# Two transposed probability tiles ahead of the next unit's scores, in the attention of the last two query groups

## The chip, the cores and the metric

The kernel runs on one core of a Trainium2 chip. The metric is the device time of one execution in microseconds (us). All tensors are float32. TensorE (PE) multiplies, VectorE (DVE) and ScalarE (ACT) do the element work, GpSimd (POOL) helps a little, SyncE (SP) issues the loads.

## The reference

Two blocks follow each other on 2048 tokens of width 1024. The change touches only the attention of the second block, which is, cut to what matters:

```python
# q_lat: (tokens, 8 heads, 128), c: latent keys (tokens, 128), w_uv: (8, 128, 64)
s_idx = ...                                  # index scores of a query against all keys
_, sel = lax.top_k(where(causal, s_idx, -inf), 256)
lg_s = q_lat @ c[sel].T * scale + rel_bias   # 8 heads
lg_m = q_lat @ c_meta.T * scale + rel_bias   # 16 meta tokens
p = softmax(concatenate([lg_m, lg_s]))
out = (p_meta @ c_meta + p_sel @ c[sel]) @ w_uv
```

The kernel doesn't gather the 256 keys: it computes the scores against all keys up to the query's block and adds a mask (`sel`, 0 or -1e30) that leaves out the keys that are not chosen.

## The kernel before, in words

The program is written out by hand, engine by engine, and the engines meet by semaphores alone. The 2048 tokens go in four groups of 512 queries (`g` = 0 to 3), each of four blocks of 128 queries (block `i` = 4g to 4g+3). For every group the second block's projections and scans run first (`second_steps`), then the attention, then the output projection.

The attention of a group is a loop over 32 **units**: a unit is one block `i` and one of 8 heads `h`. Block `i` has 128(i+1) keys, so a unit of block 8 is 1152 keys wide and one of block 15 is 2048 wide. A unit passes these stations:

1. PE: the scores S. `far` tiles of up to 512 keys (L1920) and a `near` tile of the last 256 keys (L1924). Each goes to one PSUM bank. The first head of a block is preceded by eight small products for the meta tokens (`score_m`, L1914).
2. DVE: it adds mask or bias while it copies a tile to `probs` and takes the maximum (L1530, L1537), then reduces the maxima and writes their negative to `stat` (L1544, L1545). After that it does one part of the key selection of the next block (`beside`).
3. ACT: one exp over the whole row, in place in `probs`, with the row's sum (L1058 and the read of the accumulator behind it). The semaphore `probs2_made` is raised by the last of them.
4. PE: transposes of the probabilities, 128 keys at a time, up to four to a PSUM tile (`p2_t`, L1944). A unit has `prob_tiles(i)` such tiles: 3 for blocks 8 to 11 and 4 for blocks 12 to 15. They are called T0, T1, T2, T3 here.
5. ACT: it copies each transposed tile to `prob_t` (L1052).
6. PE: the value products (L1952), called V0 to V3 here. Vc needs the copy of Tc.

The units are pipelined by one. In iteration `u` PE first computes the scores of unit `u`, then does stations 4 and 6 for unit `u-1` in the order T0, T1, V0, T2, V1, (T3, V2,) and the last V. ACT goes through the copies of unit `u-1` and then the exp of unit `u`; it takes its instructions in the order written. At two places in a block's turn there is more in an iteration: the transpose and product for the meta tokens (`pm_t`, L1930 and L1932) when a block ended two units earlier, and the transposes of the finished output (`o2_t`, four at L1966) when it ended three units earlier.

PSUM has six banks for tiles (`RING = 6`), given out in one fixed order over the whole program (`schedule`, here `dsa_tiles`). `claim` makes PE wait until the tile six places before was drained. `prob_t` has three slots (`PT_SLOTS = 3`).

Of the kernel before, what the change touches and what calls it, by code (L numbers as in the profile page):

```python
# [220 lines left out]
def keys_of(i):  # L221
    return (i + 1) * P
# [25 lines left out]

def prob_tiles_before(i, h):
    return H2 * sum(prob_tiles(b) for b in range(i)) + h * prob_tiles(i)  # L250
# [25 lines left out]
def dsa_tiles(g):  # L276
    units = dsa_units(g)
    for u in range(len(units) + 4):
        if u < len(units):
            i, h = units[u]  # L280
            if h == 0:
                yield ("score_m", i)
            yield from [("far", i, h, c) for c in range(len(far_chunks(i)))]
            yield ("near", i, h)
        if ended(units, u, 2) is not None:
            yield ("pm_t", ended(units, u, 2))
        if 1 <= u <= len(units):
            i, h = units[u - 1]
            yield from [("p2_t", i, h, c) for c in range(prob_tiles(i))]
# [70 lines left out]
def program(nc, A, out_t):  # L360
# [9 lines left out]
    with ctx:  # L370
# [410 lines left out]
        def _(act):  # L781
# [145 lines left out]

            def act_level(g, pair, lev):
# [6 lines left out]
            for g in range(G):  # L935
# [103 lines left out]
                for u in range(len(units) + 4):  # L1039
                    if ended(units, u, 2) is not None:  # L1040
# [3 lines left out]
                    if 1 <= u <= len(units):  # L1044
                        i, h = units[u - 1]
                        for c in range(prob_tiles(i)):
                            m = prob_tiles_before(i, h) + c
                            wide_ = min(TB, keys_of(i) - c * TB)
                            wait_tile(act, "p2_t", i, h, c)
                            if m >= PT_SLOTS:  # L1050
                                act.wait_ge(pv2_done, m - PT_SLOTS + 1)
                            drains(A_(prob_t[:, m % PT_SLOTS, 0:wide_], bank("p2_t", i, h, c)[:, 0:wide_], ACT.Copy), "p2_t", i, h, c)  # L1052
# [522 lines left out]
        def _(pe):  # L1575
# [221 lines left out]
            for g in range(G):  # L1797
# [107 lines left out]
                units = dsa_units(g)  # L1905
                for u in range(len(units) + 4):
                    if u < len(units):
# [25 lines left out]
                    if 1 <= u <= len(units):  # L1933
                        i, h = units[u - 1]
                        n = H2 * BG * g + u - 1
                        pe.wait_ge(probs2_made, n + 1)
                        if h == 0 and i >= 2:
                            pe.wait_ge(o2_scaled, i - 1)
                        count = prob_tiles(i)

                        def transposes2(c):
                            claim("p2_t", i, h, c)
                            for k in range(c * BG, min(c * BG + BG, i + 1)):
                                ins = nc.tensor.transpose(bank("p2_t", i, h, c)[:, (k % BG) * P:(k % BG + 1) * P],  # L1944
                                                          probs[:, (n % 2) * S + k * P:(n % 2) * S + (k + 1) * P], ident[:])
                            ins.then_inc(tile_ready, 1)

                        def values2(c):
                            wait_drained(pe, "p2_t", i, h, c)
                            m = prob_tiles_before(i, h) + c  # L1950
                            for k in range(c * BG, min(c * BG + BG, i + 1)):
                                ins = M(o_acc[i % 2][:, h * DH2:(h + 1) * DH2], prob_t[:, m % PT_SLOTS, (k % BG) * P:(k % BG + 1) * P],  # L1952
                                        v2[:, k, h * DH2:(h + 1) * DH2], start=(h == 0 and k == 0), stop=False, skip_group_check=True)
                            ins.then_inc(pv2_done, 1)

                        transposes2(0)
                        for c in range(1, count):
                            transposes2(c)
                            values2(c - 1)
                        values2(count - 1)  # L1960
# [117 lines left out]
```

## Time and profile before

| | |
|---|---|
| median of three runs | 4444.76 us (4441.53 to 4445.15) |
| the profiled execution | 4463.69 us, of which the span from first to last instruction is 4461.9 us |
| PE busy | 3973.0 us, 89% of the span |
| PE's weight loads (PEld) | 2294.7 us, 51% |
| DVE busy | 1802.1 us, 40% |
| ACT busy | 1477.2 us, 33% |
| mean granted TensorE clock | 0.932 |
| attention of group 2 (32 units) | from about 3345 to 3562 us of the span |
| attention of group 3 (32 units) | from about 4073 to 4353 us of the span |

A row of the timeline gives the start in us from the span's start, the time taken, the engine, the line, the operation, what it writes and reads, how many instructions are merged in the row, and in brackets how long the engine had been idle and who released it. A float32 matrix product stands as two instructions, so "x8" at L1952 is four value products and "x8" at L1944 is the eight transposes of T0 and T1. PE overlaps instructions, and the ends are modelled; so the text reads starts against starts.

### The profile page before, as it was taken

Reading aid. Unit: us, or ns where it says so; the run is one execution under the profiler, and the core shown is the slowest. Engines: PE = TensorE matmul, PEld = TensorE weight load, DVE = VectorE, ACT = ScalarE, POOL = GpSimd, SP = SyncE. Lnnn points to the kernel's source line nnn. Section 1 sums busy time; section 2 is a strip of 40 time slices with the busy share of each in tenths; the row PEclk is TensorE's granted clock in tenths of the full one; section 3 lists DMA queues with packets and bytes.
Section 4 is the critical chain, followed back from the end, with each engine's and each line's share of the span. In section 5 each row is a group of like instructions: output and inputs, shape, how many; then the busy total and the mean of one; then the engine's idle time right before and its main releaser. Section 6 shows DMA issues by size and latency. Waiting matters only on the chain.

```text
span 4461.9 us, 41285 instructions
## 1 busy us (share of the span) xinstructions
PE 3973.0 (89%) x15538; PEld 2294.7 (51%) x15538; DVE 1802.1 (40%) x4182; ACT 1477.2 (33%) x2457; POOL 268.7 (6%) x328
## 2 busy tenths in 40 slices
PE   7899999999999999799789787897889997687996
PEld 3346645644664464354554445644447743345773
DVE  3313222322322221227422576425776414777631
ACT  1213222312331231212312454314664413675441
POOL 0010001000000100011101011001011001011000
PEclk8999999999999999799699898998889998898998
DMA  4120022013002200411022010111100111010001
GB/s 145 57 94 6 15 78 73 1 48 106 13 10 66 71 1 19 139 50 52 1 86 75 26 48 1 62 57 50 47 19 1 58 57 52 22 48 1 1 24 53
DMA packets 70920, 204.16 MB, mean 46 GB/s; under 512 B 6297, under 2 KB 7873, under 8 KB 70465
## 3 DMA queue, kind: packets, MB, share of 16 engines
q1 hardware_dynamic: 61344, 183.67, 12.3%
q10 hardware_dynamic: 9376, 17.84, 1.1%
q8 instruction: 125, 2.05, 0.2%
q14 instruction: 75, 0.61, 0.0%
HBM read 184.69 MB, written 16.79 MB: 45 GB/s over the span
## 4 chain that ended last, share of the span: by engine, by line
PE 75%; ACT 11%; DVE 9%; issue 3%; DMA 1%; SPq 0%; POOL 0%; ACTq 0%; DVEq 0%; POOLq 0%
PE bank L1593 32%; PE o_acc L1952 6%; PE o_acc L1720 5%; PE bank L1688 5%; ACT ql L925 4%; PE bank L1920 4%; PE bank L1692 3%; PE bank L1815 3%; PE bank L1713 2%; PE bank L1944 2%; PE bank L1601 2%; PE bank L1850 2%; ACT prob_t L1052 2%; PE bank L1640 1%; PE bank L1924 1%
## 5 line engine op out<-in xcount | busy, mean ns | idle before, releaser
L1593 PE MATMUL bank<-group_even,weights 128*128 128x512 f32 x1376 | 610.3, 602 | 20.3 <-DMA weights<-in_w_in_kv 12.3
L1593 PE MATMUL bank<-group_odd,weights 128*128 128x512 f32 x1376 | 612.3, 603 | 9.4 <-ACT tmp L912 5.9
L1593 PE MATMUL bank<-y_all,weights 128*128 128x512 f32 x1024 | 452.2, 604 | 14.6 <-DMA weights<-in_w_out 8.2
L1593 PEld LDWEIGHTS bank<-group_even,weights 128*128 128x128 f32 x1376 | 264.3, 194 | 345.6 <-issue 341.3
L1593 PEld LDWEIGHTS bank<-group_odd,weights 128*128 128x128 f32 x1376 | 265.3, 195 | 337.4 <-issue 333.1
L1593 PEld LDWEIGHTS bank<-y_all,weights 128*128 128x128 f32 x1024 | 197.8, 194 | 264.3 <-issue 264.3
L1952 PE MATMUL o_acc<-v,prob_t 128*128 128x64 f32 x2176 | 293.2, 283 | 45.4 <-ACT prob_t L1052 45.4
L1178 DVE CUSTOM_DVE_ANT_0 probs<-bank,mask 128x512 f32<-128x512 f32 x256 | 161.6, 687 | 417.8 <-PE bank L1692 417.8
L1952 PEld LDWEIGHTS o_acc<-v,prob_t 128*128 128x128 f32 x2176 | 271.9, 198 | 79.9 <-ACT prob_t L1052 79.9
L1052 ACT ACTIVATE prob_t<-bank 128x512 f32<-128x512 f32 (+3 forms) x320 | 160.2, 532 | 398.9 <-PE bank L1944 398.9
L867 ACT ACTIVATE prob_t<-bank 128x512 f32<-128x512 f32 x256 | 145.9, 596 | 430.3 <-PE bank L1713 430.3
L1720 PE MATMUL o_acc<-val,prob_t 128*128 128x128 f32 x2048 | 270.3, 280 | 16.0 <-ACT prob_t L867 16.0
L1720 PEld LDWEIGHTS o_acc<-val,prob_t 128*128 128x128 f32 x2048 | 247.3, 191 | 31.2 <-ACT prob_t L867 31.2
L1530 DVE CUSTOM_DVE_ANT_0 probs<-bank,sel 128x512 f32<-128x512 f32 (+3 forms) x256 | 147.6, 595 | 227.3 <-PE bank L1920 223.9
L1688 PE MATMUL bank<-k_nope,q_nope 128*128 128x512 f32 x512 | 230.7, 593 | 0.0
L1920 PE MATMUL bank<-c_t,ql 128*128 128x512 f32 (+3 forms) x512 | 215.4, 549 | 10.3 <-DVE s_meta L1520 7.0
L1944 PE MATMUL bank<-ident,probs 128*128 128x128 f32 x1088 | 164.2, 282 | 27.7 <-ACT probs L1058 27.7
L925 ACT ACTIVATE ql<-index,mids 128x384 bf16<-128x384 f32 (+2 forms) x144 | 133.3, 927 | 124.2 <-DVE mids L1359 113.2
L1850 PE MATMUL bank<-probs 128*128 128x128 f32 x640 | 102.0, 326 | 77.8 <-DVE probs L1419 75.3
L1944 PEld LDWEIGHTS bank<-ident,probs 128*128 128x128 f32 x1088 | 136.9, 151 | 50.6 <-ACT probs L1058 30.0
L1058 ACT ACTIVATE probs<-probs,stat 128x128 f32<-128x128 f32 (+15 forms) x128 | 153.2, 1197 | 24.6 <-DVE stat L1545 23.9
L1850 PEld LDWEIGHTS bank<-probs 128*128 128x128 f32 x640 | 96.4, 236 | 104.4 <-DVE probs L1419 92.9
(340 smaller groups left out, 5002.5 us busy)
## 6 DMA issues: line engine op xcount, KB each, us to landing
weights<-in_w_in SPq DMA_DIRECT2D x101, 512.0 KB, 3.5
weights<-in_w_in_q SPq DMA_DIRECT2D x64, 512.0 KB, 3.5
weights<-in_w_out SPq DMA_DIRECT2D x64, 512.0 KB, 3.5
weights<-in_w_i SPq DMA_DIRECT2D x20, 512.0 KB, 3.5
group_even<-in_x_t SPq DMA_DIRECT2D x8, 1024.0 KB, 7.9
group_odd<-in_x_t SPq DMA_DIRECT2D x8, 1024.0 KB, 9.0
group_even<-x_t SPq DMA_DIRECT2D x8, 1024.0 KB, 8.0
group_odd<-x_t SPq DMA_DIRECT2D x8, 1024.0 KB, 7.3
```

Source lines behind the costliest of these rows:

```text
L925: A_(tested_act[:, m % 2, 0:share], index_of(BG * g + b)[:, n - share:n], ACT.Sign, scale=-1.0, bias=mids[:, b, r:r + 1], accum_out=signs[ ...
L1052: drains(A_(prob_t[:, m % PT_SLOTS, 0:wide_], bank("p2_t", i, h, c)[:, 0:wide_], ACT.Copy), "p2_t", i, h, c)
L1058: A_(p, p, ACT.Exp, bias=stat[:, 8 + n % 2:9 + n % 2], accum_out=sums2[:, i % 2, h:h + 1]).then_inc(probs2_made, 1)
L1178: drains(V.tensor_tensor_reduce(out=probs[:, (n % 2) * S + c * TB:(n % 2) * S + (c + 1) * TB], in0=bank("score", i, h, c)[:], in1=mask[:, ...
L1530: drains(V.tensor_tensor_reduce(out=probs[:, base + at:base + at + wide_], in0=bank("far", i, h, c)[:, 0:wide_], in1=sel[:, i % 2, at:at + ...
L1593: ins = M(bank(*name)[:], ring[n % SLOTS][:, k * P:(k + 1) * P], rhs[:, k, :], start=(k == 0), stop=(k == chunks - 1))
L1688: M(bank("score", i, h, c)[:], q_nope[:, h, b * P:(b + 1) * P], k_nope[:, h, c * TB:(c + 1) * TB], start=True, stop=False)
L1720: ins = M(o_acc[i % 2][:, h * P:(h + 1) * P], prob_t[:, m % PT_SLOTS, k * P:(k + 1) * P], val[:, c * BG + k, h * P:(h + 1) * P], start=(c ...
L1850: ins = M(bank(*st, e)[:, cols], keys[:, e, cols], queries[:, e, cols], start=True, stop=True)
L1920: M(bank("far", i, h, c)[:, 0:wide_], query, c_t[:, at:at + wide_], start=True, stop=True).then_inc(tile_ready, 1)
L1944: ins = nc.tensor.transpose(bank("p2_t", i, h, c)[:, (k % BG) * P:(k % BG + 1) * P], probs[:, (n % 2) * S + k * P:(n % 2) * S + (k + 1) * ...
L1952: ins = M(o_acc[i % 2][:, h * DH2:(h + 1) * DH2], prob_t[:, m % PT_SLOTS, (k % BG) * P:(k % BG + 1) * P], v2[:, k, h * DH2:(h + 1) * DH2], ...
```

## The change

For blocks 8 to 15, which are the attention of groups 2 and 3, a number `lead_of(i)` of 2 is introduced (0 for the earlier blocks, which stay as they were). In iteration `u`, PE now waits for the probabilities of unit `u-1` first and makes T0 and T1; then come the scores of unit `u`; then V0, T2, V1, V2 (three tiles) or V0, T2, V1, T3, V2, V3 (four). No instruction is added or dropped. The order in which PSUM banks are given out, and the place of the `pm_t` copy among ACT's copies, follow.

```diff
+def lead_of(i):
+
+    return 2 if i >= 2 * BG else 0
...
 def dsa_tiles(g):
     units = dsa_units(g)
     for u in range(len(units) + 4):
+        if 1 <= u <= len(units):
+            i, h = units[u - 1]
+            yield from [("p2_t", i, h, c) for c in range(prob_tiles(i))][:lead_of(i)]
         if u < len(units):
...
         if 1 <= u <= len(units):
             i, h = units[u - 1]
-            yield from [("p2_t", i, h, c) for c in range(prob_tiles(i))]
+            yield from [("p2_t", i, h, c) for c in range(prob_tiles(i))][lead_of(i):]
...
@@ ACT
                 for u in range(len(units) + 4):
+                    if 1 <= u <= len(units):
+                        for c in range(lead_of(units[u - 1][0])):
+                            transposed(*units[u - 1], c)
                     if ended(units, u, 2) is not None:
...
                     if 1 <= u <= len(units):
-                        i, h = units[u - 1]
-                        for c in range(prob_tiles(i)):
...
+                        for c in range(lead_of(units[u - 1][0]), prob_tiles(units[u - 1][0])):
+                            transposed(*units[u - 1], c)
@@ PE
                 for u in range(len(units) + 4):
+                    if 1 <= u <= len(units):
+                        i, h = units[u - 1]
+                        pe.wait_ge(probs2_made, H2 * BG * g + u)
+                        for c in range(lead_of(i)):
+                            transposes2(u - 1, c)
                     if u < len(units):
...
                     if 1 <= u <= len(units):
                         i, h = units[u - 1]
-                        n = H2 * BG * g + u - 1
-                        pe.wait_ge(probs2_made, n + 1)
                         if h == 0 and i >= 2:
                             pe.wait_ge(o2_scaled, i - 1)
...
+                        count, lead = prob_tiles(i), lead_of(i)
+                        if lead == 0:
...
+                        else:
+                            for c in range(lead, count):
+                                values2(u - 1, c - lead)
+                                transposes2(u - 1, c)
+                            for c in range(count - lead, count):
+                                values2(u - 1, c)
```

In groups 0 and 1, where `lead_of` is 0, the instructions keep their order, but the wait for `probs2_made` of unit `u-1` now stands ahead of the scores of unit `u` there too. Before, it stood behind them. On PE at a unit of block 0 the program before has, with the semaphores that an instruction waits for:

```order
L1924 MATMUL bank<-c_t,ql 128x128 [waits drained5]
L1944 MATMUL bank<-ident,probs 128x128 [waits drained0,probs2_made]
L1952 MATMUL o_acc<-v,prob_t 128x64 [waits drained0]
L1924 MATMUL bank<-c_t,ql 128x128 [waits drained1]
L1944 MATMUL bank<-ident,probs 128x128 [waits drained2,probs2_made]
L1952 MATMUL o_acc<-v,prob_t 128x64 [waits drained2]
```

and the changed one:

```order
L1962 MATMUL bank<-c_t,ql 128x128 [waits drained5,probs2_made]
L1926 MATMUL bank<-ident,probs 128x128 [waits drained0]
L1935 MATMUL o_acc<-v,prob_t 128x64 [waits drained0]
L1962 MATMUL bank<-c_t,ql 128x128 [waits drained1,probs2_made]
L1926 MATMUL bank<-ident,probs 128x128 [waits drained2]
L1935 MATMUL o_acc<-v,prob_t 128x64 [waits drained2]
```

The wait for `probs2_made` went from the transpose (L1944) up to the scores (L1962 in the new file); nothing else moved there.

On PE, in the middle of block 14 of group 3, the order before is this. L1920 and L1924 are the scores, L1944 the transposes (x8 is T0 and T1), L1952 the value products.

```order
L1920 MATMUL bank<-c_t,ql 128x512 x3
L1920 MATMUL bank<-c_t,ql 128x128
L1924 MATMUL bank<-c_t,ql 128x256
L1944 MATMUL bank<-ident,probs 128x128 x8
L1952 MATMUL o_acc<-v,prob_t 128x64 x4
L1944 MATMUL bank<-ident,probs 128x128 x4
L1952 MATMUL o_acc<-v,prob_t 128x64 x4
L1944 MATMUL bank<-ident,probs 128x128 x3
L1952 MATMUL o_acc<-v,prob_t 128x64 x7
```

At the same place the changed program has this. Its L1926 is the transposes, L1935 the value products, L1958 and L1962 the scores.

```order
L1926 MATMUL bank<-ident,probs 128x128 x8
L1958 MATMUL bank<-c_t,ql 128x512 x3
L1958 MATMUL bank<-c_t,ql 128x128
L1962 MATMUL bank<-c_t,ql 128x256
L1935 MATMUL o_acc<-v,prob_t 128x64 x4
L1926 MATMUL bank<-ident,probs 128x128 x4
L1935 MATMUL o_acc<-v,prob_t 128x64 x4
L1926 MATMUL bank<-ident,probs 128x128 x3
L1935 MATMUL o_acc<-v,prob_t 128x64 x7
```

The scores moved from ahead of T0 to between T1 and V0. So what lies between the scores of a unit and its own T0 is now one row of values less the scores of another unit, and what lies between T0 and V0 is more by those scores.

At the start of group 3's attention PE has this before (L1914 is the meta tokens' scores of block 12).

```order
L1914 MATMUL bank<-c_meta,ql 128x16 x8
L1920 MATMUL bank<-c_t,ql 128x512 x2
L1920 MATMUL bank<-c_t,ql 128x384
L1924 MATMUL bank<-c_t,ql 128x256
L1920 MATMUL bank<-c_t,ql 128x512 x2
L1920 MATMUL bank<-c_t,ql 128x384
L1924 MATMUL bank<-c_t,ql 128x256
L1944 MATMUL bank<-ident,probs 128x128 x8
L1952 MATMUL o_acc<-v,prob_t 128x64 x4
```

And in the changed program, where L1952 is the meta tokens' scores:

```order
L1952 MATMUL bank<-c_meta,ql 128x16 x8
L1958 MATMUL bank<-c_t,ql 128x512 x2
L1958 MATMUL bank<-c_t,ql 128x384
L1962 MATMUL bank<-c_t,ql 128x256
L1926 MATMUL bank<-ident,probs 128x128 x8
L1958 MATMUL bank<-c_t,ql 128x512 x2
L1958 MATMUL bank<-c_t,ql 128x384
L1962 MATMUL bank<-c_t,ql 128x256
L1935 MATMUL o_acc<-v,prob_t 128x64 x4
```

The scores of the group's second unit stood ahead of the first transposes; now they stand behind them. Group 2 starts in the same way.

## Rows read from the trace of the kernel before

**Rows 1.** Timeline of one unit of block 15 in group 3.

```profile
4318.48 3.23 PE L1920 MATMUL bank<-c_t,ql 128*128 128x512 f32 x8
...
4321.97 1.04 PE L1944 MATMUL bank<-ident,probs 128*128 128x128 f32 x8
...
4323.02 0.15 DVE L1545 TENSOR_SCALAR stat<-m 128x1 f32<-128x1 f32 x1
4323.26 1.10 PE L1952 MATMUL o_acc<-v,prob_t 128*128 128x64 f32 x8 [0.25 <-ACT prob_t L1052]
...
4324.20 0.60 PE L1944 MATMUL bank<-ident,probs 128*128 128x128 f32 x4
4324.64 1.00 PE L1952 MATMUL o_acc<-v,prob_t 128*128 128x64 f32 x8
...
4325.48 0.61 PE L1944 MATMUL bank<-ident,probs 128*128 128x128 f32 x4
...
4326.62 1.99 ACT L1058 ACTIVATE probs<-probs,stat 128x2048 f32<-128x2048 f32 x1
4327.72 1.51 PE L1920 MATMUL bank<-c_t,ql 128*128 128x512 f32 x3
```

**Rows 2.** Timeline of one unit of block 8 in group 2.

```profile
3378.57 1.10 PE L1952 MATMUL o_acc<-v,prob_t 128*128 128x64 f32 x8 [0.25 <-ACT prob_t L1052]
...
3380.69 1.72 PE L1920 MATMUL bank<-c_t,ql 128*128 128x512 f32 x4
3381.14 0.19 ACT L1058 ACTIVATION_READ_ACCUMULATOR probs<-probs,stat 128x1 f32 x1
```

**Rows 3.** Timeline of one unit of block 12 in group 3.

```profile
4117.24 1.10 PE L1952 MATMUL o_acc<-v,prob_t 128*128 128x64 f32 x8 [0.25 <-ACT prob_t L1052]
...
4120.64 1.94 PE L1920 MATMUL bank<-c_t,ql 128*128 128x512 f32 x4
4121.52 0.19 ACT L1058 ACTIVATION_READ_ACCUMULATOR probs<-probs,stat 128x1 f32 x1
```

**Rows 4.** Timeline of group 3's last unit, which no further scores precede.

```profile
4341.74 1.10 PE L1952 MATMUL o_acc<-v,prob_t 128*128 128x64 f32 x8 [0.25 <-ACT prob_t L1052]
...
4346.99 0.19 ACT L1058 ACTIVATION_READ_ACCUMULATOR probs<-probs,stat 128x1 f32 x1
...
4347.23 1.09 PE L1944 MATMUL bank<-ident,probs 128*128 128x128 f32 x8 [0.88 <-ACT probs L1058]
...
4348.57 0.66 PE L1952 MATMUL o_acc<-v,prob_t 128*128 128x64 f32 x4 [0.25 <-ACT prob_t L1052]
```

**Rows 5.** Timeline of PE in the first two units of group 2.

```profile
3351.51 1.97 PE L1944 MATMUL bank<-ident,probs 128*128 128x128 f32 x8 [2.52 <-ACT probs L1058]
...
3353.31 1.97 PE L1952 MATMUL o_acc<-v,prob_t 128*128 128x64 f32 x8
...
3357.31 3.30 PE L1920 MATMUL bank<-c_t,ql 128*128 128x512 f32 x4
...
3361.09 1.04 PE L1944 MATMUL bank<-ident,probs 128*128 128x128 f32 x8
```

**Rows 6.** Timeline of PE in the first unit of group 3.

```profile
4078.19 1.10 PE L1944 MATMUL bank<-ident,probs 128*128 128x128 f32 x8 [0.57 <-ACT probs L1058]
```

**Rows 7.** Timeline between two units of block 0 in group 0.

```profile
2182.36 0.74 PE L1924 MATMUL bank<-c_t,ql 128*128 128x128 f32 x2
2182.45 0.19 ACT L1058 ACTIVATION_READ_ACCUMULATOR probs<-probs,stat 128x1 f32 x1
```

**Rows 8.** Timeline between two units of block 4 in group 1.

```profile
2748.21 0.20 ACT L1058 ACTIVATION_READ_ACCUMULATOR probs<-probs,stat 128x1 f32 x1
2748.66 0.86 PE L1920 MATMUL bank<-c_t,ql 128*128 128x384 f32 x2
```

**Rows 9.** Two stretches: PE, PEld, DVE, ACT, POOL busy (x), clock, DMA share, GB/s.

```profile
4080.00:4352.00 272.00, 262.30 (x1715) 207.21 (x1714) 139.30 (x408) 124.91 (x195) 15.43 (x24) 1.00 0.04 13
2732.00:2897.00 165.00, 146.72 (x847) 111.19 (x846) 76.06 (x278) 60.20 (x130) 15.32 (x24) 0.93 0.11 39
```

More of the change, by code:

```diff
@@ L926, in signs_of, with transposed @@
                        accum_out=signs[:, b, r:r + 1]).then_inc(signs_summed, 1)
+            def transposed(i, h, c):
+                m = prob_tiles_before(i, h) + c
+                wide_ = min(TB, keys_of(i) - c * TB)
+                wait_tile(act, "p2_t", i, h, c)
+                if m >= PT_SLOTS:
+                    act.wait_ge(pv2_done, m - PT_SLOTS + 1)
+                drains(A_(prob_t[:, m % PT_SLOTS, 0:wide_], bank("p2_t", i, h, c)[:, 0:wide_], ACT.Copy), "p2_t", i, h, c)
             def act_level(g, pair, lev):
@@ L1905, in _, with transposes2, values2 @@
                 units = dsa_units(g)
-                for u in range(len(units) + 4):
+                def transposes2(u, c):
+                    i, h = units[u]
+                    n = H2 * BG * g + u
+                    claim("p2_t", i, h, c)
+                    for k in range(c * BG, min(c * BG + BG, i + 1)):
+                        ins = nc.tensor.transpose(bank("p2_t", i, h, c)[:, (k % BG) * P:(k % BG + 1) * P],
+                                                  probs[:, (n % 2) * S + k * P:(n % 2) * S + (k + 1) * P], ident[:])
+                    ins.then_inc(tile_ready, 1)
+                def values2(u, c):
+                    i, h = units[u]
+                    wait_drained(pe, "p2_t", i, h, c)
+                    m = prob_tiles_before(i, h) + c
+                    for k in range(c * BG, min(c * BG + BG, i + 1)):
+                        ins = M(o_acc[i % 2][:, h * DH2:(h + 1) * DH2], prob_t[:, m % PT_SLOTS, (k % BG) * P:(k % BG + 1) * P],
+                                v2[:, k, h * DH2:(h + 1) * DH2], start=(h == 0 and k == 0), stop=False, skip_group_check=True)
+                    ins.then_inc(pv2_done, 1)
+                for u in range(len(units) + 4):
+                    if 1 <= u <= len(units):
[3 more added lines that the diff above has]
+                            transposes2(u - 1, c)
                     if u < len(units):
@@ L1934, in _ @@
                         i, h = units[u - 1]
-                        n = H2 * BG * g + u - 1
-                        pe.wait_ge(probs2_made, n + 1)
                         if h == 0 and i >= 2:
                             pe.wait_ge(o2_scaled, i - 1)
[L1939 to L1960, printed above, removed]
+                        count, lead = prob_tiles(i), lead_of(i)
+                        if lead == 0:
+                            transposes2(u - 1, 0)
+                            for c in range(1, count):
+                                transposes2(u - 1, c)
+                                values2(u - 1, c - 1)
+                            values2(u - 1, count - 1)
+                        else:
+                            for c in range(lead, count):
+                                values2(u - 1, c - lead)
+                                transposes2(u - 1, c)
+                            for c in range(count - lead, count):
+                                values2(u - 1, c)
                     over = ended(units, u, 3)
```

6 lines of the change are left out of this document (removed).

## The prediction

> **What bounds the kernel now.** I read the table of busy times first, then the timeline of single units in each group's attention, then the busy table of whole stretches. PE is the engine to watch: it is busy 89% of the span, and in group 3's attention (the stretch from 4080) 262.3 of 272 us, with the clock at 1.00 [rows 9]. A unit of block 15 shows the whole turn, read start to start [rows 1]: scores 4318.48 to 4321.97 (3.49 us), T0 and T1 up to V0 at 4323.26 (1.29), then V0, T2, V1, T3, V2, V3 up to the next scores at 4327.72 (4.46), 9.24 us in all. PE's one wait in it is at V0, for ACT's copy of T0: 0.25 us idle, in blocks 8 and 12 as well [rows 1 to 3]. The exp of the scores just made starts at 4326.62, behind the copy of T3, and runs on into PE's next scores; nobody waits for it. So two latencies stand in a unit: the copy of T0, which PE sees, and the exp, which the next scores cover.
>
> **The change part by part.** In groups 2 and 3 it exchanges the two: the scores cover the copy, and the value products alone must cover the exp. In groups 0 and 1 it only moves the wait for the exp ahead of the scores.
>
> *What is won in a unit of groups 2 and 3.* T2's four transposes give the bare pace, 4324.20 to 4324.64 = 0.44 us, so T0 and T1 take 0.88 where 1.29 pass now: 0.41 won. V0, begun after a stall, takes 0.94 up to T2, while V1 takes 0.84, 4324.64 to 4325.48 [rows 1]: 0.10 more won, as V0 will follow the scores without a pause. Together 0.51.
>
> *What is lost there.* T0 of the next unit comes straight after the last V. It needs the exp, and the exp comes behind the copy of the last T, since ACT takes its work in order; that copy hangs on V0's start in the same iteration, so I measure from there. The trace already has this order once in each group: behind the last unit's T and V there are no further scores. In block 15, V0 starts at 4341.74, the exp is done at 4346.99 + 0.19 = 4347.18, and T0 starts at 4347.23, 0.05 later and 5.49 after V0 [rows 4]. The T and V work ends 4.46 after V0 [rows 1]: the wait is 1.03. In block 12 the exp is done 4.47 after V0 (4121.71), the work at 3.40 [rows 3]; with the 0.05 the wait is 1.12. In block 8 it is 2.76 (3381.33) + 0.05 against 2.12 [rows 2]: 0.69. T0 after a wait has its first weights to load: 1.34 to V0, against 1.29 [rows 4, 1], so 0.05 more. I take the mean of the ends for group 3, 1.08, and for group 2, with the same fall of 0.09 over its blocks, 0.65.
>
> *Counts.* A group has 32 units. The last gap before T0 waits already, and the first unit is costed below; this leaves 30 waits in group 3. In group 2 the half clock at the start, where V and T take 4.00 us [rows 5], covers the exp once more, which leaves 29. Waits: 30 x 1.08 + 29 x 0.65 = 51.3. At six places the four transposes of `o2_t` (0.44, by T2's pace) lie in the gap: -2.6. At six block changes the exp is 128 keys wider, 1.99 x 128 / 2048 = 0.12 [rows 1]: +0.7. That makes +49.4. Won: 59 x (0.51 - 0.05) = -27.1. Together +22.3.
>
> *The starts of groups 2 and 3.* The scores of unit 1 were made while PE waited for the first exp; now they follow it. In group 2 the clock is at half after the pause: T0 and T1 take 1.80, and block 8's scores 3.78, 3357.31 to 3361.09 [rows 5], where full clock would give 3.49 x 1152/2048 = 1.96. In the new order: T0 at 3351.51, scores from 3353.3, V0 at 3357.1, T0 of unit 1 at 3361.1, then at full clock 0.93 and 1.96, V0 at 3364.0. Now that V0 comes 1.29 after 3361.09: +1.6. In group 3 PE was busy with unit 1's scores ahead of T0 at 4078.19 [rows 6], so V0 came after a normal 1.3. Now PE idles until T0, so T0, T1 and block 12's scores follow a pause as in group 2: at full clock 0.93 + 2.84, at half 1.80 + 5.5, that is +2.4 or +5.9. Group 2's rows, whose scores six us behind the pause still took twice their time, are the nearer: +5.0.
>
> *Groups 0 and 1.* In block 0 the exp is done at 2182.45 + 0.19 = 2182.64, while the scores behind it start at 2182.36 [rows 7]. With 0.05 they will start 0.33 later, and DVE and ACT, which set this turn, don't catch up: 7 x 0.33 = 2.3. In block 4 the exp is done at 2748.41 and the scores start at 2748.66 [rows 8]: 0.20 to spare, no cost. At both groups' starts unit 1's scores are uncovered as above; by width at half clock that is about 0.6 in group 0 and 2.1 in group 1. With 0.2 for other places of group 0, +5.2. If the 0.20 of group 1 were gone and 0.1 missing, 31 units would cost 3.1 more.
>
> *Costed at nothing.* PSUM banks: with 6, 8 or 9 tiles to a unit, the tile six places before is always one that DVE or ACT took before the exp in question or during the scores. DVE in groups 2 and 3: `stat` is ready 1.20 us after the scores' end, which is T0's start now (4323.17 against 4321.97) and V0's in the new order; the exp starts 3.36 after V0 in block 15 [rows 1]. In block 8 it starts 1.4 after V0 (its end, 2.76, less 1.3), so the cover is 0.1 to 0.2; each 0.1 that is missing costs up to 6 us over 60 units. DVE's selection part behind `stat` has the exp, T0, T1 and the first scores to hide in, over 3 us even in block 8. `pm_t` and its wait stand ahead of V0 as before.
>
> *Sum.* 22.3 + 1.6 + 5.0 + 5.2 = +34.1 us. On the profiled execution this is 4463.7 + 34.1 = 4497.8; the runs' median is 18.9 lower, so 4444.8 + 34.1 = **4478.9 us**, 0.77% slower.
>
> **A rule against the change.** In group 3's attention the clock is at 1.00 with PE busy 96%; in group 1's (from 2732), where PE is busy 146.7 of 165 us, 89%, it is 0.93 [rows 9]. The new waits bring groups 2 and 3 to about 88%. With two levels, a mean of 0.93 is half clock for 14% of the time. The Trainium skill, TensorE: Matmul & The Clock Gate, section on the second HAM failure mode, says that PE idling briefly but often between groups of products makes the clock swing between its levels. By that rule the loss would be larger than my sum; group 1's row agrees with it, group 3's doesn't contradict it. What it would do here is the second rival.
>
> **The rivals.**
> 1. *As summed*: 4478.9, between 4468 and 4490 from the start in group 3 and the small terms. Chance 0.67.
> 2. *The clock falls too.* With group 1's 0.93, 14% of 470 us, 66 us, pass at half, which costs about half of it, +33: 4512; if the clock falls only at the block changes, +5 to +20. I put it at 4500. For it: the busy share. Against it: the scores here are wider than group 1's. Chance 0.15.
> 3. *DVE or ACT is late as well*, by 0.2 to 0.3 us a unit in the narrow blocks, where the spare is 0.1 to 0.2: +10 to +18, about 4493. Chance 0.05.
> 4. *The waits are smaller than I read them*, half of 1.08 and 0.65 or so, if the turn settles at another phase: 25 us less, 4454. Against it: the trace has the new order at 4347.23, with just the wait computed [rows 4]. Chance 0.08.
> 5. *The other side: the copy's wait goes and nothing takes its place.* The exp would have to be done within the V and T work, so to start at least 1.03 us sooner in block 15, ahead of T3's copy. Then 59 x 0.51 = 30.1 are won and 11.8 lost at the starts and in group 0: 4426. It is a gain from a mean wait below 0.26 (59 x 0.26 = 27.1 - 11.8). Against it is ACT's order, which has the exp last. Chance 0.05.
>
> **How the numbers follow.** The predicted time is the first case's. The range 4465 to 4502 takes in its own range, most of the third and half of the second; the fourth, the fifth and the worst of the clock stay outside, about 0.2. A measurement of this kernel can tell 0.2%, 9 us, from no change. Faster is the fifth case, 0.05; same is part of the fourth, 0.04; slower is the rest, 0.91.
>
> **What the profile after would show.** At the transposes' line the exp (ACT `probs`) should stand as PE's releaser about 60 times, with 0.9 us idle in group 3 and about 0.5 in group 2 (idle by the page, 0.88 at 4347.23 for 1.03 start to start [rows 4]). The wait for `prob_t` at V0 should be left in groups 0 and 1 and at the last units. A unit of block 15 should last 9.24 + 1.03 + 0.05 - 0.51 = 9.81 us, of block 12 0.66 more than now, of block 8 0.23 more. In block 0 the scores should wait for the exp, in block 4 not. The clock should be 1.00 in groups 2 and 3 apart from their starts. Another releaser, or a clock that falls inside a group, would make the prediction wrong.

## The result and the profile after

The changed kernel took 4496.95 us in the median of four executions (4482.10 to 4499.11), against 4444.95 us for the kernel before beside it: ratio 1.0111, 95% interval 1.0089 to 1.0134. It is slower, by 52 us where 34 were forecast. A second comparison, told below, gave 1.0072 (1.0050 to 1.0095), 32 us; of its ten executions of the change one took 13905.6 us, at a mean granted clock of 0.394, and is left out. The profiled execution took 4482.10 us, span 4480.3.

The page after, PE's busy row and clock row first, then two groups (busy, mean ns | idle before, and its releaser):

```profile
PE 3957.1 (88%) x15538; PEld 2292.7 (51%) x15538; DVE 1802.3 (40%) x4182; ACT 1478.3 (33%) x2457; POOL 268.7 (6%) x328
...
PEclk9999999999999999789699899998889998888998
...
L1935 PE MATMUL o_acc<-v,prob_t 128*128 128x64 f32 x2176 | 281.3, 277 | 30.4 <-ACT prob_t L943 30.4
...
L1926 PE MATMUL bank<-ident,probs 128*128 128x128 f32 x1088 | 167.8, 286 | 71.2 <-ACT probs L1072 71.0
```

PE's waits from 3330 to 4400, the attention of groups 2 and 3 and what lies between (us in total, times, longest):

```profile
PE bank L1926 <- ACT probs L1072: 71.0, 61, 14.6
...
PE o_acc L1935 <- ACT prob_t L943: 0.5, 2, 0.3
```

The exchange is in these two rows. The wait for the copy at the value products (L1935) is gone but for two, 0.5 us in all; in its place stand 61 waits for the exp at the transposes (L1926). The longest of them, 14.6 and 13.7, are the two group starts, where PE waited before as well, though partly with scores in between.

Timeline of a unit of block 15, which answers to [rows 1]:

```profile
4333.04 1.00 PE L1935 MATMUL o_acc<-v,prob_t 128*128 128x64 f32 x8
4333.88 0.61 PE L1926 MATMUL bank<-ident,probs 128*128 128x128 f32 x4
...
4335.81 0.60 ACT L943 ACTIVATE prob_t<-bank 128x512 f32<-128x512 f32 x1 [0.69 <-PE bank L1926]
4336.30 1.99 ACT L1072 ACTIVATE probs<-probs,stat 128x2048 f32<-128x2048 f32 x1
4338.19 0.19 ACT L1072 ACTIVATION_READ_ACCUMULATOR probs<-probs,stat 128x1 f32 x1
4338.44 1.09 PE L1926 MATMUL bank<-ident,probs 128*128 128x128 f32 x8 [0.88 <-ACT probs L1072]
...
4339.37 3.17 PE L1958 MATMUL bank<-c_t,ql 128*128 128x512 f32 x8
...
4342.81 1.00 PE L1935 MATMUL o_acc<-v,prob_t 128*128 128x64 f32 x8
```

Read start to start: V0 to the next T0 takes 5.40 us. V0 now takes 0.84 like V1, so the T and V work is 4.36, and PE waits 1.04. T0 starts 0.06 after the exp's read of the accumulator ends (4338.38). T0 and T1 take 0.93, the scores 3.44, and V0 follows at 4342.81 with no wait: the copies of T0 and T1, 1.08 us from 4339.13, are done while the scores run. The turn is 9.77 us, where [rows 1] gave 9.24.

The same in block 12 (V0, then T0 behind its wait):

```profile
4112.57 1.00 PE L1935 MATMUL o_acc<-v,prob_t 128*128 128x64 f32 x8
...
4117.00 1.09 PE L1926 MATMUL bank<-ident,probs 128*128 128x128 f32 x8 [0.97 <-ACT probs L1072]
```

And in block 8:

```profile
3370.30 1.00 PE L1935 MATMUL o_acc<-v,prob_t 128*128 128x64 f32 x8
...
3373.02 1.09 PE L1926 MATMUL bank<-ident,probs 128*128 128x128 f32 x8 [0.54 <-ACT probs L1072]
```

The start of group 3's attention, which answers to [rows 6]:

```profile
4073.98 1.97 PE L1926 MATMUL bank<-ident,probs 128*128 128x128 f32 x8 [14.55 <-ACT probs L1072]
...
4075.74 3.95 PE L1958 MATMUL bank<-c_t,ql 128*128 128x512 f32 x6
...
4079.96 1.00 PE L1935 MATMUL o_acc<-v,prob_t 128*128 128x64 f32 x8
```

PE stood still for 14.55 us, T0 and T1 then took 1.76, twice the pace of 0.88, and the scores 4.22, between the 2.84 of full and the 5.5 of half clock: the clock came back while they ran. V0 is 5.98 us behind T0, where it was 1.3 behind. So the start costs 4.7.

The start of group 2's attention, which answers to [rows 5]:

```profile
3342.18 1.97 PE L1926 MATMUL bank<-ident,probs 128*128 128x128 f32 x8 [13.71 <-ACT probs L1072]
3343.94 3.19 PE L1958 MATMUL bank<-c_t,ql 128*128 128x512 f32 x4
...
3347.78 1.18 PE L1935 MATMUL o_acc<-v,prob_t 128*128 128x64 f32 x8
...
3350.68 1.09 PE L1926 MATMUL bank<-ident,probs 128*128 128x128 f32 x8 [0.54 <-ACT probs L1072]
```

V0 comes 5.60 us behind T0, all of it at half clock (0.50 from 3342 to 3348). From 3348 to 3349 the granted clock is 0.93, so the V and T work behind it runs at full clock, and T0 of the next unit follows 2.90 after V0, behind a wait.

Between two units of block 0, which answers to [rows 7]:

```profile
2180.95 0.19 ACT L1072 ACTIVATION_READ_ACCUMULATOR probs<-probs,stat 128x1 f32 x1
2181.19 0.79 PE L1962 MATMUL bank<-c_t,ql 128*128 128x128 f32 x2
```

The exp ends at 2181.14 and the scores start 0.05 later. The turn is 2.19 us (these scores start at 2181.19, the next at 2183.38), against 1.80 before. In block 4 it is 3.58 as before.

Two stretches after, of groups 3 and 2 (columns as in [rows 9]):

```profile
4100.00:4360.00 260.00, 233.91 (x1505) 185.98 (x1506) 121.95 (x360) 110.31 (x172) 15.43 (x24) 0.99 0.00 1
3365.00:3550.00 185.00, 171.12 (x1118) 137.76 (x1118) 94.29 (x308) 80.82 (x141) 15.40 (x24) 1.00 0.04 12
```

From its first exp to its last, group 2 lasts 211.1 us (206.9 before) and group 3 293.4 (268.7 before). Together that is 28.9 us more.

### The profile page after: what moved, and what is told of

Read it like the earlier page. It is cut to its first block, busy times and chain, and to the rows that moved or that the text cites. A ratio compares the mean times of both kernels' runs of the same rounds, so it can differ in the third digit from the quotient of the medians.

```text
span 4480.3 us, 41299 instructions
## 1 busy us (share of the span) xinstructions
PE 3957.1 (88%) x15538; PEld 2292.7 (51%) x15538; DVE 1802.3 (40%) x4182; ACT 1478.3 (33%) x2457; POOL 268.7 (6%) x328
## 4 chain that ended last, share of the span: by engine, by line
PE 73%; ACT 12%; DVE 10%; issue 3%; DMA 1%; SPq 0%; POOL 0%; DVEq 0%; ACTq 0%; POOLq 0%
PE bank L1607 31%; PE o_acc L1734 5%; PE bank L1702 5%; ACT ql L933 5%; PE bank L1958 4%; PE o_acc L1935 3%; PE bank L1926 3%; PE bank L1706 3%; PE bank L1829 3%; ACT probs L1072 2%; PE bank L1727 2%; PE bank L1615 2%; PE bank L1864 2%; PE bank L1654 1%; PE bank L1962 1%
## 5 line engine op out<-in xcount | busy, mean ns | idle before, releaser
L1935 PE MATMUL o_acc<-v,prob_t 128*128 128x64 f32 x2176 | 281.3, 277 | 30.4 <-ACT prob_t L943 30.4
L1935 PEld LDWEIGHTS o_acc<-v,prob_t 128*128 128x128 f32 x2176 | 272.1, 195 | 55.3 <-ACT prob_t L943 49.4
L1926 PE MATMUL bank<-ident,probs 128*128 128x128 f32 x1088 | 167.8, 286 | 71.2 <-ACT probs L1072 71.0
L1958 PE MATMUL bank<-c_t,ql 128*128 128x512 f32 (+3 forms) x512 | 210.9, 541 | 13.2 <-ACT probs L1072 13.2
L1926 PEld LDWEIGHTS bank<-ident,probs 128*128 128x128 f32 x1088 | 132.6, 151 | 92.6 <-ACT probs L1072 81.0
L1727 PE MATMUL bank<-ident,probs 128*128 128x128 f32 x1024 | 146.1, 275 | 3.3 <-ACT probs L880 3.3
```

The lines of the kernel that those rows point to most:

```text
L1727: ins = nc.tensor.transpose(bank(*name)[:, k * P:(k + 1) * P], probs[:, col:col + P], ident[:])
L1958: M(bank("far", i, h, c)[:, 0:wide_], query, c_t[:, at:at + wide_], start=True, stop=True).then_inc(tile_ready, 1)
```

## The experiments

Two theories stood against each other. **The chain**: V0, the T's that follow it, the copy of the last of them, then the exp, then the next T0, and PE waits for what its own work doesn't cover. **The clock**: the new waits, in groups 0 and 1 above all, bring the granted clock down, which would explain the surplus of the first comparison over the sum. A turn below is the time from the start of one exp to the start of the next; a steady turn is one away from a group's start and from the changes of block.

**The wait moved, without the lead.** In every group the wait for the exp stands ahead of the scores, and the tiles stay where they were.

```diff
-    return 2 if i >= 2 * BG else 0
+    return 0
```

> The change without its main part: no tile goes ahead in any group, but the wait for the exp stands ahead of the next unit's scores in all four groups. If unhidden exps are what costs (theory A), groups 2 and 3 pay the same here as in the change, without what V0 wins: per unit S, T, V and then a wait. From V0 the exp is done as before (5.49 us in block 15, 4.52 in block 12, 2.81 in block 8 against 4.46, 3.40, 2.12), so about +1.0, +1.1 and +0.7 a unit, +50 us in groups 2 and 3, +5 in groups 0 and 1 and +10 at the starts: +60 us, 1.35%. If it was the exchange with the copy's wait that mattered (theory B: the order of T and S as such costs), this kernel should be near the one before, +5 to +10.

Measured: 4528.4 us (4 executions), ratio 1.0177 (1.0153 to 1.0202), the kernel before on this chip at 4450.8. PE in block 15 of that kernel, two waits in one turn:

```profile
4345.14 1.10 PE L1935 MATMUL o_acc<-v,prob_t 128*128 128x64 f32 x8 [0.25 <-ACT prob_t L943]
...
4350.64 2.84 PE L1958 MATMUL bank<-c_t,ql 128*128 128x512 f32 x6 [0.88 <-ACT probs L1072]
```

Both latencies stand open here: 5.50 from V0 to the scores, and the copy's 0.25 besides. The steady turns are 6.15 us in block 8 and 10.33 in block 15, against 5.59 and 9.77 in the changed kernel. So the lead of two tiles wins 0.56 us a unit (0.51 forecast), and the exp's wait costs 0.75 to 1.17 with what hangs on it (block 8 and 12). The change as a whole is the lead's gain less a larger loss.

The time is more than was expected: 1.35% lies below the interval. Groups 2 and 3 last 234.9 and 317.6 us from first exp to last, 76.9 more than in the kernel before. Of these, 16.8 stand in eight turns that are 1.7 or 3.4 us longer than at full clock; behind the starts the two groups have 34 us at half clock. Two stretches behind the starts (columns as in [rows 9], granted clock 0.96):

```profile
4125.00:4385.00 260.00, 230.17 (x1385) 173.64 (x1384) 115.81 (x340) 99.90 (x156) 15.42 (x24) 0.96 0.00 1
3365.00:3550.00 185.00, 166.54 (x998) 126.78 (x998) 85.98 (x276) 71.94 (x127) 15.44 (x24) 0.96 0.04 12
```

So with both waits open the clock did fall inside the groups. The profile is one, but all four executions lie above 4526 us. What is left, 60 us, is what was expected of the groups and their starts (50 and 10).

**The lead, without the moved wait in groups 0 and 1.**

```diff
-                        pe.wait_ge(probs2_made, H2 * BG * g + u)
+                        if lead_of(i) > 0:
+                            pe.wait_ge(probs2_made, H2 * BG * g + u)
...
+                        if lead_of(i) == 0:
+                            pe.wait_ge(probs2_made, H2 * BG * g + u)
```

> The change without its side effect: T0 and T1 go ahead in groups 2 and 3, and in groups 0 and 1 the wait for the exp is where it was. Theory A by the prediction's terms: groups 2 and 3 cost 22.3 + 6.6 = +29 us, and in groups 0 and 1 nothing, so 5 us less than the change. Theory C says that what the change's median has over the sum (52 against 34 us) is the clock in groups 0 and 1, pushed to its lower level by the moved wait in block 0: then this kernel is about 20 us faster than the change, near +29 with a group 0 like the one before. If the excess comes from groups 2 and 3, it stays near +47.

Measured: 4478.4 us (6 executions), ratio 1.0063 (1.0039 to 1.0088). Groups 2 and 3 have the turns of the changed kernel to 0.01 us, block 0 has its 1.80 again. The ratio's 28 us are near the 29 that the chain gave. By itself this spoke for the clock theory too, since it lies 18.6 us below the first median of the change. The next two runs speak otherwise.

**The changed kernel again, in more executions.**

> The changed kernel itself, with more runs, beside the moved wait alone and on the chip of the other experiments. If what exceeded the sum (52 us measured against 34 forecast) was chance in the clock of single runs, the median comes near 4451 + 34 = 4485 us (ratio 1.0077). If the moved wait in groups 0 and 1 costs through the clock, it stays near 4497 us (ratio 1.011), that is 18 us above the kernel that has the same order in groups 2 and 3 but the old wait in groups 0 and 1 (4478.4).

Measured: 4482.8 us, ratio 1.0072 (1.0050 to 1.0095), from nine executions of 4472.6 to 4498.8. That is near the expected 1.0077, and 0.0009 above the lead alone. The first comparison's four executions of the change, and its four of the kernel before, lie within the range of the single executions here, the highest 0.3 us above it, so its surplus can be chance; a difference between the chips that the two ran on isn't excluded.

**The moved wait in groups 0 and 1 alone**, the rest as before.

```diff
-    return 2 if i >= 2 * BG else 0
+    return 0
...
-                        pe.wait_ge(probs2_made, H2 * BG * g + u)
+                        if i < 2 * BG:
+                            pe.wait_ge(probs2_made, H2 * BG * g + u)
...
+                        if i >= 2 * BG:
+                            pe.wait_ge(probs2_made, H2 * BG * g + u)
```

> The kernel before, with the wait for the probabilities moved ahead of the scores in groups 0 and 1 alone; groups 2 and 3 stay as they were. By the prediction's sum: +5.2 us, ratio 1.0012 (block 0's unit 2.19 instead of 1.80, the first scores of the two groups uncovered). If this wait pulls the clock down as well: +15 to +20 us, ratio 1.0035 to 1.0045, with more of group 0 and 1 at half clock in the profile.

Measured: 4457.5 us (12 executions) against 4452.4, ratio 1.0007 (0.9989 to 1.0026). In block 0 the first turn rose from 1.23 to 2.09, the five steady ones from 1.80 to 2.19 and the one into block 1 from 5.88 to 6.27, 3.15 us over the block. The clock theory's 1.0035 to 1.0045 is outside the interval: as an explanation of the surplus it falls. The forecast 5.2 us are inside, and so is no cost at all.

The moved wait does change where the clock is low, though. In the five profiles that have it (this one, the one without the lead, two of the changed kernel and, below, one with half of the exp) group 0 lasts 103.5 to 106.1 us from first exp to last and group 1 145.5 to 152.0. In the eight with the old wait group 0 lasts 91.2 to 115.1, and group 1 152.2 in seven and 147.3 in one. The two groups together take 249.0 to 258.0 us (252.9 in the mean) against 243.5 to 266.0 (252.2).

**Second profiles of both kernels.**

> A second profile of the changed kernel. Its steady units should be the same within 0.01 us (5.59, 8.15, 9.77), as they belong to the order; what differs from the first profile (span 4480.3) should stand in the stretches at half clock alone: near the beginning of each group's attention, at block changes and in blocks 1 and 2.

> A second profile of the kernel before. Its steady units should be the same within 0.01 us (5.40, 7.54, 9.24); its span may differ from 4461.9 by 10 to 25 us, all of it at half clock in groups 0 and 1 and at block changes, if the spread from run to run is the clock's.

Measured: the change 4486.5 us (span 4484.6), the kernel before 4447.3 (span 4445.5, 16.4 less than in its first profile). The steady turns of both agree with their first profiles within 0.01 us. In the kernel before, group 0's attention in the first profile:

```profile
2174.00:2265.00 91.00, 77.19 (x315) 58.95 (x316) 39.79 (x181) 27.18 (x84) 16.55 (x27) 0.61 0.07 24
```

The same stretch in the second profile:

```profile
2174.00:2265.00 91.00, 74.09 (x391) 56.73 (x390) 46.04 (x212) 33.91 (x97) 15.41 (x24) 0.81 0.08 25
```

One program, one stretch of 91 us, and once 315 and once 391 matmul instructions done, at a clock of 0.61 and 0.81. From first to last exp group 0 lasts 105.3 and 91.3 us, which is 14.0 of the 16.4 us between the spans. In group 3 of the changed kernel two stretches at half clock, at 4208 and 4218, make the turns at two block changes 12.38 and 12.51 us long; the second profile has 10.70 and 10.84 there, and 1.68 more in two other turns. The kernel before has such turns as well (10.19 for 8.49 and 11.24 for 9.54 in its second profile). They aren't the change's alone, but it may bring more of them. In groups 2 and 3, behind the half clock of the starts, four profiles with the old order have none, two, none and one (the kernel before twice, the moved wait in groups 0 and 1 alone, and the kernel before with half of the exp, below). Both profiles of the changed kernel and that of the lead alone have two, and the kernel with the first units in the old order, also below, has three, one of them 10.2 us long. So few profiles don't settle it, and at 1.7 us for 3.4 at half clock it is little.

**Half of the exp, in the changed kernel and in the kernel before.** Both leave out half of the exponentials.

```diff
-                        p = probs[:, (n % 2) * S:(n % 2) * S + keys_of(i)]
+                        p = probs[:, (n % 2) * S:(n % 2) * S + (keys_of(i) if i < 2 * BG else (i + 2) // 2 * P)]
...
+                    return k if i < 2 * BG else k // 2
```

> The changed kernel with the exp over about half of the row in groups 2 and 3 (blocks 8 to 15; the transposes read that half twice), so it leaves out half of the exponentials. The exp is shorter by 0.82 ns a key: 0.42 us in block 8, 0.63 in block 12, 0.84 in block 15. If PE's wait is for the end of the exp, the units shrink by just that, to 5.17, 7.52 and 8.93 us, and the waits for the exp to 0.27, 0.49 and 0.19; some 37 us in all. If the wait came from the copies or from DVE, the units would stay at 5.59, 8.15 and 9.77.

> The control for the half exp: the kernel before with the exp over about half of the row in groups 2 and 3 (blocks 8 to 15), so it leaves out half of the exponentials. Before the change PE's next scores cover the exp, so the units should stay at 5.40 (block 8), 7.54 (block 12) and 9.24 us (block 15), within 0.03, and groups 2 and 3 at 206.9 and 268.7 us from first to last exp, apart from the clock. If the exp's length counts in any order, they shrink by 0.4 to 0.8 us as in the changed kernel.

Measured: 4447.9 us and 4457.8 us, one execution each. Block 15 in the changed kernel with half the exp:

```profile
4310.19 1.00 PE L1938 MATMUL o_acc<-v,prob_t 128*128 128x64 f32 x8
...
4313.45 1.14 ACT L1072 ACTIVATE probs<-probs,stat 128x1024 f32<-128x1024 f32 x1
4314.49 0.19 ACT L1072 ACTIVATION_READ_ACCUMULATOR probs<-probs,stat 128x1 f32 x1
4314.74 1.09 PE L1929 MATMUL bank<-ident,probs 128*128 128x128 f32 x8
```

V0 to T0 is 4.55 us now, by 0.85 less than the 5.40, and the exp is shorter by just that (1.14 for 1.99). The turns are 5.16, 7.51 and 8.91 us in blocks 8, 12 and 15, where 5.17, 7.52 and 8.93 were expected. In the kernel before, the same shortening changes nothing:

```profile
4324.67 0.19 ACT L1058 ACTIVATION_READ_ACCUMULATOR probs<-probs,stat 128x1 f32 x1
4324.73 3.23 PE L1920 MATMUL bank<-c_t,ql 128*128 128x512 f32 x8
```

The exp and its read are done 0.13 us after the scores start, over 3 us before the T0 that needs them, and the turns stay at 5.40, 7.54 and 9.24. So the exp's length counts in the new order only. Each kernel has one execution, but the turns repeat to 0.01 us, and this pair shows what the main loss is: PE waits for the end of the exp.

**The first unit of groups 2 and 3 in the old order**, on top of the lead-only kernel.

```diff
-def lead_of(i):
+def lead_of(i, h=1):
...
-    return 2 if i >= 2 * BG else 0
+    return 2 if i >= 2 * BG and (i % BG, h) != (0, 0) else 0
...
```

> As e2_lead_only, but the first unit of each block row of groups 2 and 3 keeps the old order (its T0 and T1 stay behind the next unit's scores), only at the two group starts. Theory A: the scores of unit 1 are covered by the wait for the first exp again, which the prediction put at 1.6 us in group 2 and 5.0 in group 3, less 0.5 for V0's wait each: 5 to 6 us faster than e2_lead_only. If the clock is not lower behind the pause for being idle longer, only 3 us.

Measured: 4486.8 us (6 executions), ratio 1.0076 (1.0049 to 1.0103). Its start of group 3:

```profile
4077.93 3.35 PE L1959 MATMUL bank<-c_t,ql 128*128 128x512 f32 x4 [7.01 <-DVE s_meta L1534]
...
4082.71 1.09 PE L1926 MATMUL bank<-ident,probs 128*128 128x128 f32 x8 [0.57 <-ACT probs L1072]
...
4084.05 1.10 PE L1935 MATMUL o_acc<-v,prob_t 128*128 128x64 f32 x8 [0.25 <-ACT prob_t L943]
```

With unit 1's scores in front, T0 finds the clock up, and V0 comes 1.34 behind it instead of 5.98. The first turn is 5.89 instead of the changed kernel's 10.42 us: 4.5 saved, beside 1.5 in group 2's first three. Against the lead-only kernel, on which it is built, it is 5.4 over the first two turns (14.04 for 19.42) and 1.0 in group 2. In the median nothing of it shows; the profile has 3.4 us at half clock at 3505, 3.4 at 4140 and 10.2 at 4212, where the lead-only profile had 3.4 at 4079 and 3.4 at 4185. The interval holds both a gain of 5 us and none, so in the time of the kernel it is inconclusive; in the trace the start is as forecast.

**Three tiles ahead in group 3**, two in group 2, on top of the lead-only kernel.

```diff
-    return 2 if i >= 2 * BG else 0
+    return 3 if i >= 3 * BG else 2 if i >= 2 * BG else 0
```

> The lead-only kernel with three transposed tiles ahead of the next scores in group 3 (two in group 2). Then only T3 follows V0, its copy ends about 2.1 us after V0 in block 15 and about 1.4 in block 12, and the exp starts there instead of about 3. If the wait comes from the exp's place behind the last copy, it falls from 1.03 to 0.41 in block 15 and from 1.12 to 0.46 in block 12: units of 9.19 and 7.49 us (9.77 and 8.15 in the lead-only kernel), some 19 us less over group 3, time about 4459 us. If something else than the copy holds the exp (DVE's stat, a fixed turn), the units stay at 9.77 and 8.15 and the time at 4478.

Measured: 4450.4 us (12 executions) against 4452.4, ratio 0.9980 (0.9958 to 1.0002). Block 15 there:

```profile
4299.41 0.61 PE L1926 MATMUL bank<-ident,probs 128*128 128x128 f32 x4
...
4300.05 0.60 ACT L943 ACTIVATE prob_t<-bank 128x512 f32<-128x512 f32 x1 [4.02 <-PE bank L1926]
4300.55 1.99 ACT L1072 ACTIVATE probs<-probs,stat 128x2048 f32<-128x2048 f32 x1
...
4302.69 1.53 PE L1926 MATMUL bank<-ident,probs 128*128 128x128 f32 x12
```

One row of values less stands ahead of the last copy, so the exp starts 1.98 after V0 (0.84 to T3 and 1.14 from there) instead of 3.26, and T0 comes 4.12 after V0 instead of 5.40. The turns are 7.31 and 8.92 us in blocks 12 and 15. Expected were 7.49 and 9.19; I had taken 1.24 from T3 to the exp, and had added the exp and the read of its accumulator (2.18) where they overlap (2.08). That is 0.20 of the 0.27 in block 15. Had something else than the copies held the exp, the turns would have stayed at 8.15 and 9.77. The order of the change, then, isn't slower in itself. With two tiles ahead the exp is late, with three it is nearly in time, and group 3 is faster than before (264.3 for 268.7 us), though the interval of the whole kernel still holds no difference. That it is the place of the exp behind the last copy that decides is shown by this.

**The copy's wait covered by T2 instead**, from the kernel before: T0, T1, T2, V0, (T3,) V1 and so on in groups 2 and 3; nothing precedes the scores.

```diff
-                        transposes2(0)
-                        for c in range(1, count):
-                            transposes2(c)
-                            values2(c - 1)
-                        values2(count - 1)
+                        ahead = 3 if i >= 2 * BG else min(count, 2)
+                        for c in range(ahead):
+                            transposes2(c)
+                        for c in range(ahead, count):
+                            values2(c - ahead)
+                            transposes2(c)
+                        for c in range(count - ahead, count):
+                            values2(c)
```

> The kernel before with one other order: scores first as before, then T0, T1 and T2, then V0 (T3, V1, V2, V3) in groups 2 and 3. T2's four transposes (0.44 us, in block 8 one, 0.11) fill the wait for the copy of T0 (0.41), and the exp keeps the scores as its cover. Theory A: V0's wait goes in blocks 11 to 15 (0.41 + 0.10 a unit), about two thirds of it in block 10, half in block 9 and a quarter in block 8, while the last T's copy may then be what the last V waits for: 40 x 0.45 + 24 x 0.25 = 24 us won, -0.5%. If a new wait takes its place (the copies are 0.55 each and come one after the other, so V1 and V2 may wait for theirs), the gain is under 10 us.

> The kernel before with T0, T1 and T2 ahead of V0 in groups 2 and 3, again, with more runs: by its units in the first profile (0.06 less in block 8 to 0.45 less in block 15) about 20 us less than the kernel before, ratio 0.9955; 0.9965 was measured, and by the chance of single runs the new ratio should lie between 0.994 and 0.998.

Measured: 4444.3 against 4450.8 us, ratio 0.9965 (0.9941 to 0.9990), and 4434.7 against 4456.2, ratio 0.9958 (0.9933 to 0.9984), 12 executions each. The 24 us first expected are 0.9946, just inside the first interval. Block 15, V0 with no wait ahead of it and the scores with none either:

```profile
4301.04 3.23 PE L1920 MATMUL bank<-c_t,ql 128*128 128x512 f32 x8
...
4304.53 1.47 PE L1944 MATMUL bank<-ident,probs 128*128 128x128 f32 x12
...
4305.84 1.08 PE L1952 MATMUL o_acc<-v,prob_t 128*128 128x64 f32 x8
...
4309.83 0.65 PE L1920 MATMUL bank<-c_t,ql 128*128 128x512 f32 x1
```

Three tiles at 0.44 take 1.31, hardly more than the 1.29 that two tiles and the wait took in [rows 1]. The turn is 8.79 us instead of 9.24, and 5.34 instead of 5.40 in block 8. This version is faster than the kernel before by 0.4%, and so than the changed one, which ran slower than the kernel before in both comparisons.

## Why the prediction was right, point by point

The mechanism was right: PE waits for the exp at the next T0, by what was read from the last unit of the old trace, and pays more there than it wins at V0. Some of the terms were not, and they are named below.

**What is won in a unit.** Forecast 0.41 and 0.10, less 0.05 for T0 behind a wait. Measured: T0 to V0 less the scores is 0.93 for 1.29, V0 takes 0.84 for 0.94, and the scores, 3.44 for 3.49, give 0.05 that I had not counted. The lead against the moved wait alone is 0.56.

**What is lost.** The waits of 1.03, 1.12 and 0.69 in blocks 15, 12 and 8 are the heart of the sum. Measured by V0 to T0 they are 5.40 (forecast 5.49 less 0.10), 4.43 (4.52 less 0.10) and 2.72 (2.81 less 0.10). The last unit's order in the old trace [rows 4] did foretell the new one.

**The turns.** Forecast 9.81 in block 15, 0.66 more in block 12, 0.23 more in block 8; measured 9.77, 0.61 and 0.19 (5.59 for 5.40). The small difference is the scores' 0.05. Over the groups' blocks the excess is 0.19, 0.18, 0.17, 0.10 and 0.61, 0.60, 0.60, 0.53. The `o2_t` transposes lie in the gap, as counted: the turns that were 0.40 longer for them before (6.34 for 5.94) are as long as the others now (6.12).

**The starts.** Group 3: forecast +5.0, measured +4.7 by the trace and 4.5 by the experiment. Group 2: forecast +1.6; the first three turns, 19.10 us before, are 19.68 after, and of these 0.58 some 0.4 are steady excess, so the term was too large by over 1 us. T0 to V0 took 5.60, as forecast (1.80 and 3.78), but the clock was back 0.4 us behind V0: the V and T work that I had taken at half clock, 4.00 us by [rows 5], ran at full. Group 1: forecast +2.1, and this term did not come at all. The first two turns of block 4 are 5.01 and 3.59 against 4.69 and 4.26: the half clock after the pause ended 4.4 us behind the group's first exp, where it had lasted 8.6. Why it ended sooner isn't shown.

**Groups 0 and 1.** Forecast 0.33 a turn in block 0, the 0.05 behind the exp included; measured 0.39. The missing 0.06 is in the scores themselves: begun behind a wait, they have DVE start 0.93 us after them (2181.19 to 2182.12), where it was 0.87 (2180.56 to 2181.43), and the whole turn hangs on DVE and ACT. With the start that is 3.15 us; block 4 kept its turn. The whole part measured 0.07%, 3 us, against 5.2 forecast, in an interval from 5 us less to 12 more.

**The sum.** In the two profiles of the change groups 2 and 3 last 28.9 and 27.5 us longer than in the first profile of the kernel before, and 25.6 and 24.2 longer than in its second. That the first figure is the forecast's 22.3 + 1.6 + 5.0 = 28.9 is luck: 3.4 of it are the two stretches at half clock, and without them it is 25.5. With 3.2 for block 0 the terms measure 28.7, 5.4 less than the 34.1 of the sum: 2.1 in group 1's start, 1.4 in group 2's, 0.5 in group 3's, and the rest, some 1.5, in the turns. In time, the 13 executions of the change in the two comparisons have a median of 4483.4 us, the 65 of the kernel before in all comparisons 4452.4, which is 31.0 apart. The median of 4496.95 lay 18 us above the forecast 4478.9 and was inside its range by the room left for a falling clock and for a late DVE or ACT, of which the profiles of the changed kernel show little or nothing. The forecast also started from a median of 4444.8, 7.6 us below that of the 65.

**The clock.** Forecast 1.00 in groups 2 and 3 apart from their starts; measured 1.00 and 0.99, against 1.00 in the same parts of the kernel before's first profile and 0.99 in its second. The Trainium skill, TensorE: Matmul & The Clock Gate, section on the second HAM failure mode, would have brief and frequent idling swing the clock. With a wait of nearly a microsecond in each turn and PE busy 233.9 of 260 us, group 3 stayed at 0.99, with 1.7 us lost at each of two places, as in the second profile of the kernel before. So this trace doesn't bear the rule out, and the second rival, in which the clock fell as well, came in the changed kernel with 3.4 us at most. It did come in the kernel with both waits open, at 0.96 in groups 2 and 3 and 16.8 us lost. Of the others, DVE and ACT were not late (in groups 2 and 3 V0 waited twice, 0.3 us at most, and the half exp gave back its whole length), and the waits were not half of what I read.

## What to carry to other kernels

Where a pipeline has two latencies and one long stretch of cover, price both ends of an exchange from the same trace: here the copy's 0.4 us was traded for an exp whose finish hung on PE's own last tile. Look for the one place in the old trace where the new order already happens, such as the last turn of a loop, and read the wait there. And when a short latency is to be hidden, take the nearest independent work (one more transposed tile), not the work that covers something longer.

## What was not expected of the hardware

- The spread of one program is mostly the granted clock in one place. The kernel before, on several chips, took 4435.2 to 4474.9 us over 65 executions. Its group 0 lasted 105.3 and 91.3 us, and in the six other profiles whose program is the same up to there 91.2 to 115.1. The difference is in blocks 1 to 3: the seventh turn of block 1 was 1.84 us with the clock up and 2.97 with it down, the fifth of block 2 was 2.49 and 4.15.
- A comparison of four executions against four gave a ratio 0.0039 above that of nine against 27, and outside its interval.
- Short stretches at half clock, of 3.4 us, fell into turns whose PE work was nearly continuous, in both kernels, each costing 1.7 us. In the kernel with two waits in each turn they added up to 34 us in groups 2 and 3, in the changed kernel to 6.8 in each of two profiles, in the kernel before to none and 6.8.
